# Two neighbouring rows of the down weights per partition, and every second column in the activation transposes

## What is computed

```python
def expert_block(args):
    xb, e = args                                   # tokens of one expert, 1024 wide
    gu = xb @ w_gu[e] + b_gu[e]                    # 1024 x 2048
    x_glu = jnp.minimum(gu[:, :D_FF], SWIGLU_LIMIT)
    x_lin = jnp.clip(gu[:, D_FF:], -SWIGLU_LIMIT, SWIGLU_LIMIT)
    act = x_glu * jax.nn.sigmoid(SWIGLU_ALPHA * x_glu) * (x_lin + 1)
    return act @ w_down[e] + b_down[e]             # 1024 x 1024
```

## Time and profile before

| | |
|---|---|
| median of 3 runs | 1814.66 us (1814.03 to 1814.68) |
| the profiled execution's own time | 1813.89 us |
| its span, first to last instruction | 1812.2 us |
| mean granted TensorE clock | 0.971 |
| busy: PE, DVE, ACT, POOL | 92%, 75%, 62%, 21% |
| loads of gate and up weights | 256 of 1 MB |
| loads of down weights | 128 of 1 MB |

### The profile page before, as it was taken

How to read it: one execution, slowest core, us unless ns; L and a number is a source line. 1 busy time by engine, 2 the same in 40 slices (tenths; PEclk the granted TensorE clock), 3 DMA queues, 4 the chain that set the end, 5 groups by cost and what they waited for, 6 DMA issues and landing times.

```text
span 1812.2 us, 22271 instructions
## 1 busy us (share of the span) xinstructions
PE 1668.9 (92%) x7695; PEld 1299.1 (72%) x7695; DVE 1357.5 (75%) x1224; ACT 1117.5 (62%) x1035; POOL 377.3 (21%) x453
## 2 busy tenths in 40 slices
PE   7999999999988957999999999999999999999992
PEld 6877668889775736777777777777777777767761
DVE  4444562345433658899999999999999999999994
ACT  4235564235224224687887878878878888788772
POOL 5002321000000105622221221221221221221221
PEclk9999999999999978999999999999999999999996
DMA  9221223234430334999999999999999999999983
GB/s 322 89 93 59 83 81 134 94 116 163 162 96 0 118 148 157 338 382 394 390 402 392 393 403 392 391 404 391 393 401 390 396 397 391 395 397 394 396 339 107
DMA packets 110112, 497.57 MB, mean 275 GB/s; under 512 B 9365, under 2 KB 9434, under 8 KB 77194
## 3 DMA queue, kind: packets, MB, share of 16 engines
q1 hardware_dynamic: 98752, 459.30, 64.8%
q0 software_dynamic: 9824, 32.54, 7.1%
q10 hardware_dynamic: 1482, 5.01, 0.7%
HBM read 476.44 MB, written 20.38 MB: 274 GB/s over the span
## 4 chain that ended last, share of the span: by engine, by line
PE 64%; DVE 16%; issue 9%; ACT 6%; POOL 3%; DMA 2%; DVEq 0%; SPq 0%; ACTq 0%; POOLq 0%
PE ps L2107 18%; DVE wlo L1447 11%; PE ps L2127 8%; PE ps L1706 7%; PE ps L1708 7%; PE ps L1707 7%; ACT whi L1040 4%; POOL slot_table L736 2%; PE ps L1829 2%; PE ps L1831 2%; PE ps L1833 2%; PE ps L2058 2%; PE ps L1856 1%; DVE glu L1481 1%; PE ps L1897 1%
## 5 line engine op out<-in xcount | busy, mean ns | idle before, releaser
L1447 DVE TENSOR_TENSOR wlo<-raw,whi 128x2048 fp32r<-128x2048 f32 x380 | 849.9, 2287 | 60.1 <-ACT whi L1040 59.9
L1040 ACT ACTIVATE whi<-raw 128x2048 fp32r<-128x2048 f32 x380 | 709.1, 1910 | 86.0 <-PE ps L2107 82.2
L1194 DVE TENSOR_TENSOR wlo<-raw,whi 128x2048 fp32r<-128x2048 f32 x52 | 119.7, 2327 | 157.7 <-ACT whi L800 157.7
L2058 PE MATMUL ps<-whi,xhl 128*128 128x512 f32 x480 | 140.6, 415 | 33.8 <-DVE wlo L1447 31.4
L2107 PE MATMUL ps<-whi,xhi 128*128 128x512 f32 x544 | 152.2, 402 | 8.0 <-DVE wlo L1447 7.8
L2107 PE MATMUL ps<-wlo,xhi 128*128 128x512 f32 x544 | 147.2, 393 | 0.0
L2107 PE MATMUL ps<-whi,xlo 128*128 128x512 f32 x544 | 146.1, 390 | 0.0
L800 ACT ACTIVATE whi<-raw 128x2048 fp32r<-128x2048 f32 x52 | 97.9, 1916 | 71.5 <-DVE branch L1345 29.5
L2058 PEld LDWEIGHTS ps<-whi,xhl 128*128 128x128 f32 x480 | 84.9, 190 | 77.9 <-DVE wlo L1447 60.9
L2058 PE MATMUL ps<-wlo,xhl 128*128 128x512 f32 x480 | 131.1, 395 | 0.0
L2107 PEld LDWEIGHTS ps<-whi,xhi 128*128 128x128 f32 x544 | 101.7, 190 | 30.9 <-DVE wlo L1447 7.2
(11 more groups left out here) (379 smaller groups left out, 3001.1 us busy)
## 6 DMA issues: line engine op xcount, KB each, us to landing
raw<-in_w_gu SPq DMA_DIRECT2D x256, 1024.0 KB, 9.0
raw<-in_w_down SPq DMA_DIRECT2D x128, 1024.0 KB, 6.9
raw<-in_w_in SPq DMA_DIRECT2D x14, 1024.0 KB
raw<-in_w_gate SPq DMA_DIRECT2D x8, 1024.0 KB
raw<-in_w_xkv SPq DMA_DIRECT2D x8, 1024.0 KB
raw<-in_w_attn_up SPq DMA_DIRECT2D x4, 1024.0 KB
raw<-in_w_out SPq DMA_DIRECT2D x4, 1024.0 KB
raw<-in_w_xq SPq DMA_DIRECT2D x4, 1024.0 KB
```

The costliest lines, as they stand in the source:

```text
L1040: s.activation(whi[:, m % RING, :], raws[m % RAWS], ACT.Copy).then_inc(hi_done, 1)
L1194: v_.tensor_tensor(wlo[:, u % RING, :], raw[:, u % RING, :], whi[:, u % RING, :].bitcast(F32), ALU.subtract).then_inc(lo_done, 1)
L1447: v_.tensor_tensor(wlo[:, m % RING, :], raws[m % RAWS], whi[:, m % RING, :].bitcast(F32), ALU.subtract).then_inc(lo_done, 1)
L2058: mm = t_.matmul(ps[:, n, :], xhl[:, k, :], w[:, slot, n * 512:(n + 1) * 512], start=False, stop=False)
```

## The change

Each down unit still holds the same 256 rows of an expert's down matrix. Before, partition p got rows p and p+128 of them (two pieces of 4 KB that lie 512 KB apart in memory); now it gets rows 2p and 2p+1, which are neighbours and make one piece of 8 KB. To match, tile k of the turned activations is made of every second column of the 256 that belong to unit j = k // 2: the even ones for the first half of the unit and the odd ones for the second. The sum over k is the same, in another order. The piece of `hid` that PE loads for a transpose is now read with a step of two elements. No instruction is added, removed or moved on any engine.

```diff
             def down_unit(e, j, m, lo_value):
                 src = A["w_down"][0][bass.ds(e, 1), 2 * j * P:(2 * j + 2) * P, :].rearrange(
-                    "a (k p) n -> p (a k) n", p=P)
+                    "a (p k) n -> p (a k n)", p=P)
 
                 sp.wait_ge(lo_done, lo_value)
-                sp.dma_start(raws[m % RAWS].rearrange("p (k n) -> p k n", k=2), src
-                             ).then_inc(raw_landed[m % RAWS], 16)
+                sp.dma_start(raws[m % RAWS], src).then_inc(raw_landed[m % RAWS], 16)
@@
                 pe.wait_ge(x_ready, free)
+                pairs = hid[:, :].rearrange("s (j p k) -> s j k p", j=KT // 2, k=2)
                 for k in range(KT):
-                    tr = t_.transpose(ps[:, 6 + k // 4, k % 4 * P:k % 4 * P + CAP], hid[:, k * P:(k + 1) * P],
+                    tr = t_.transpose(ps[:, 6 + k // 4, k % 4 * P:k % 4 * P + CAP], pairs[:, k // 2, k % 2, :],
                                       ident[0:CAP, 0:CAP])
                 tr.then_inc(a_turned, 1)
```

## The result

| | before | changed |
|---|---|---|
| median of 14 runs each | 1815.95 us | 1820.76 us |
| lowest and highest | 1811.84, 1819.29 | 1816.32, 1823.50 |
| ratio, 95% interval | | 1.0024 (1.0016 to 1.0032) |
| the profiled execution, its span | 1813.89, 1812.2 | 1816.32, 1814.6 |

The 14 runs of before hold the three shown earlier, and the other eleven lie mostly a little above those. The ratio comes to 4.4 us, with an interval from 2.9 to 5.8. My forecast was no change, with 0.79; the measured median lies 0.26 us above the range's upper end. It is the case that the prediction had as rival one, near its cheaper price.

The account below looks back on a forecast made before the run. Pairs of experts were taken to be bound by PE in heavy stretches and ACT and DVE in light ones, not by loads. Terms -0.2 + 0 + 0 + 0 = -0.2 us gave 1814.5 us, range 1811.5 to 1820.5.

Parts of the forecast that it names:

- rival one: In the 128 chain transposes, spaced weight loads cost about 5 us (chance 0.07) or 10 us or more (0.05).
- What bounds the kernel: Expert pairs of 67.05 us: PE leads the heavy stretch, ACT and DVE the light; loads are hardly waited for.
- Packets, -0.2 us: Down loads in 8 KB packets land slightly earlier, shortening ACT's three waits: -0.2 us, bounds -2.9 to 0.
- Issue, 0: SP issues each down load in 333 ns, not 373; the saving lies beside SP's waits, so 0.
- Weight loads, 0: PE's transposes loading with a step of two cost nothing extra: 0 taken from a bracket up to 17.9 us.
- 16 groups of 8 transposes: Transposes in the chain, 15 heavy stretches and one at the end: 128 in all, one each 83 ns.
- cover for the light ones: In light stretches ACT takes the transposes' result 1.2 us after they end, so longer loads there cost nothing.
- the low end: Chain transposes: 0 ns extra each, since float32 loads of 64 and 128 columns take 134 and 140 ns.
- The bf16 row: PE's 96x128 load in bf16, half the bytes, takes 98 ns, 42 less; used to price bytes covered.
- the middle value of 5.4 us: Chain transposes: doubling the bytes covered adds 84 ns per load, half in the open, 42 ns x 128.
- Rival two: Down loads with 8 KB rows land later, making light stretches wait: 28 us, 1842 us at 11.1 us landing; chance 0.03.
- Rival three: Fewer packets ease SBUF ports for DVE and ACT in light stretches: faster than the waits allow, chance 0.06.

Follow-up runs that it names:

- e1: Kernel before with only the down loads changed to 8 KB rows, transposes still reading packed columns: 1815.42 us against 1815.96, ratio 0.9997.
- e4: Changed kernel, but VectorE reads its inputs with a step of two and writes packed, transposes read packed: 1816.09 us, ratio 0.9998 to before.
- e11: Repeat of the variant where VectorE reads with a step of two and transposes read packed, beside the changed kernel: 1816.29 us, ratio 0.9997 to before.
- e10: The changed kernel run once more, unaltered, compared with the kernel before: 1820.10 us, ratio 1.0018.
- e8: Changed kernel with only the light experts' 15 transpose groups reading every second column, the others packed: 1815.84 us against 1816.50 before, ratio 1.0004.
- e9: Kernel before with the moving operand of the heavy experts' gate and up products read every second column: 2168.55 us in one execution, 352 us over before.
- e5: Changed kernel with transposes reading every fourth column in place of every second: 1820.83 us, ratio 1.0031 to before.
- e6: Changed kernel with transposes reading every eighth column in place of every second: 1819.34 us, ratio 1.0014 to before.
- e2: Kernel before with only the transposes changed to every second column, old loads kept: 1820.47 us, ratio 1.0022.
- e3: Changed kernel, but VectorE writes even and odd columns to separate halves and transposes read packed: 1822.81 us, ratio 1.0037 to before.

## Where the prediction was right and where not

**What bounds the kernel: right.** The pairs have one period, PE holds the chain through the heavy stretch, and nobody waits for loads. e1, e4 and e11 show it: 8 KB packets, 16384 fewer of them, and no time that can be told from before's (their intervals leave room for a gain of about 2 us at most).

**Packets, -0.2 us: not told from zero.** Neither the gain nor the waits' disappearance was seen. ACT's waits for down loads were 3.4 us after and 1.9 in e10, with 2.9 before; over all kernels run they were 0.8 to 3.4 us with the new loads and 2.9 to 3.8 with the old, so a small gain isn't excluded either. The landing was forecast a little below 6.9 us; it was 7.6 here and says nothing, by the spread above.

**Issue, 0: right,** with the 333 ns that was forecast.

**Weight loads, 0: this is the step that failed.** I had the right 16 groups of 8 transposes, the right cover for the light ones (e8) and a bracket that held the truth, 0 to 17.9 us. But inside it I took the low end, "by the row that is nearest in type": 64 columns of float32 in 134 ns against 128 in 140. Those rows vary how many numbers are read, all of them packed; they say nothing of a step. By e9's rate, if it holds for loads, the 64 columns would take 29 ns and the 128 take 57, so most of both durations would not be reading at all, and a row that is mostly something else can't bound the reading. The bf16 row was no better guide. The same view of before has this row beside it, where half the columns take longer, 109 ns against 98, so that these durations don't go by the bytes:

```profile
L2062 PEld LDWEIGHTS ps<-bias,sel_gu_l 96*64 96x64 bf16 x60 | 5.4, 109 | 8.5 <-issue 5.4
```

The measured term is 33 ns x 128 = 4.2 us, close to the middle value of 5.4 us, half of 84 ns, which was right in size by luck: its reason, the bytes covered, fell with e5 and e6.

**The rivals.** Rival one was given 0.07 at about 5 us and 0.05 at 10 us or more; the cheaper part is what happened. Its sign in the profile was named (weight loads above 150 ns, each pair longer by eight times the excess); the load's own 77 ns were not the excess, since only 33 of them showed between transposes. Rival two fell with e1 and with e2, where the loads of before landed latest of all. Its ground was 6.9 against 9.0 us at the median. The down loads in the 8 KB form land at 6.7 to 7.6 us while the gate and up loads of the same form stay at 8.4 to 9.4 in every kernel but e9, so the form isn't what sets the two apart. The prediction had argued so. Rival three (faster by more than the waits give) shows in no run.

**The chances.** 0.79 for no change rested on taking an unseen operation at the value of a seen one. When a trace shows no operand with a step on PE and the priced bracket reaches 18 us over a path of 128 instructions, "0" is one choice among several. The range, too, stopped at 1820.5 by a median of before from three runs; that of all 14 lies 1.3 us higher. Without that rise the result would have lain inside the range, and the step above would have been no less wrong.

## What to carry to other kernels

Keep both operands of TensorE packed in float32: a step of two in a moving operand doubled the time of 512 columns, and in a weight load it turned 83 ns per transpose into 115. No run here has a step in a 16-bit operand. When rows must be interleaved for longer DMA pieces, let an engine that has the slack read with the step (VectorE did it in the same 1.22 us) and write packed, and first ask whether anyone waits for the DMA; here nobody did. And a change of 0.2% is read from the period of a repeated stretch, not from two spans, whose beginnings differed by several us.

## What the runs showed of the hardware that was not expected

- A moving operand of four-byte numbers (fp32r) with a step of two elements: 454 ns per 512 columns against 229, both at the 2.4 GHz level (e9). Any step of two, four or eight in a weight load of 96x128: 217, 218, 207 ns against 140.
- VectorE's float32 product of 1024 columns with two inputs read at a step of two: 1.22 us, as packed (e4). With results alternating between two places 2 KB apart: 2.07 us (e3).
- Loads of 1 MB in 128 pieces of 8 KB or 256 of 4 KB: no difference in time at a DMA share of 1.01 to 1.02, while the median to landing moved between 6.7 and 7.6 us in two executions of the same kernel.
